# An inference step on one core: expert down matrices loaded as eight consecutive rows per partition, and `hid` turned by every eighth column

## The reference

```
g, idx = lax.top_k(aff.T, cap)
xe = xt[idx]
h = silu(einsum('ecd,edf->ecf', xe, w_gate)) * einsum('ecd,edf->ecf', xe, w_up)
ye = einsum('ecf,efd->ecd', h, w_down) * g[..., None]
out = zeros_like(xt).at[idx.reshape(-1)].add(ye.reshape(-1, D))
```

## Time and profile before

| | |
|---|---|
| median of 3 runs | 2083.78 us (2082.12 to 2083.93) |
| the profiled execution | 2084.59 us |
| its span | 2082.8 us |
| mean granted TensorE clock | 0.916 |
| busy: TensorE, VectorE, ScalarE, GpSimd | 1812.0, 1544.0, 1214.7, 570.5 us |
| HBM read | 496.90 MB |
| packets of the SP queue (q1) | 124288, 484.22 MB |

### The profile page before, as it was taken

How to read it: one execution, slowest core, us unless ns; L and a number is a source line. 1 busy time by engine, 2 the same in 40 slices (tenths; PEclk the granted TensorE clock), 3 DMA queues, 4 the chain that set the end, 5 groups by cost and what they waited for, 6 DMA issues and landing times.

```text
span 2082.8 us, 26307 instructions
## 1 busy us (share of the span) xinstructions
PE 1812.0 (87%) x8919; PEld 1265.4 (61%) x8919; DVE 1544.0 (74%) x1822; ACT 1214.7 (58%) x1518; POOL 570.5 (27%) x320
## 2 busy tenths in 40 slices
PE   1599969789999999999568789898699999999996
PEld 0388847656666666666357578777366666666664
DVE  0457663479999999999346376634699999999994
ACT  0356751168777777777241145522378777777774
POOL 0122230103434444342200050000223434434331
PEclk7699979599999999999779779997799999999997
DMA  9400271799999999999760330006399999999992
GB/s 342 137 1 1 83 292 48 299 339 366 361 375 358 378 359 378 362 378 365 189 134 0 128 121 1 1 1 269 135 361 376 359 378 359 376 357 378 365 376 83
DMA packets 139904, 519.04 MB, mean 249 GB/s; under 512 B 14944, under 2 KB 15232, under 8 KB 138815
## 3 DMA queue, kind: packets, MB, share of 16 engines
q1 hardware_dynamic: 124288, 484.22, 60.4%
q0 software_dynamic: 7216, 24.79, 6.2%
q10 hardware_dynamic: 8334, 9.17, 1.4%
HBM read 496.90 MB, written 21.24 MB: 249 GB/s over the span
## 4 chain that ended last, share of the span: by engine, by line
PE 55%; DVE 19%; issue 13%; ACT 5%; DMA 4%; ACTq 2%; POOL 1%; DVEq 0%; SPq 0%; POOLq 0%
PE ps L729 19%; PE ps L733 10%; DVE whl L1482 9%; PE ps L687 5%; PE ps L931 4%; PE ps L978 2%; ACT whl L1099 2%; DVE W L1513 2%; DMA ring<-in_at_w_qkv 2%; ACTq L1188 2%; PE ps L951 2%; PE ps L967 1%; PE ps L667 1%; PE ps L761 1%; DVE W L1500 1%
## 5 line engine op out<-in xcount | busy, mean ns | idle before, releaser
L1482 DVE TENSOR_TENSOR whl<-ring,whl 128x1024 fp32r<-128x1024 f32 x768 | 970.0, 1302 | 79.3 <-ACT whl L1099 66.7
L1099 ACT ACTIVATE whl<-ring 128x1024 fp32r<-128x1024 f32 x768 | 805.5, 1059 | 253.1 <-PE ps L733 234.9
L729 PE MATMUL ps<-whl,xs_hl 128*80 128x512 f32 x2048 | 561.0, 396 | 7.3 <-DVE xs_hl L1506 3.8
L729 PEld LDWEIGHTS ps<-whl,xs_hl 128*80 128x80 f32 x2048 | 298.7, 149 | 169.4 <-issue 6.2
L733 PE MATMUL ps<-whl,xs_hl 128*80 128x512 f32 x1024 | 323.3, 397 | 10.8 <-DVE whl L1482 7.5
L729 PE MATMUL ps<-whl,hs_hl 128*80 128x512 f32 x1024 | 280.9, 396 | 3.4 <-ACT hs_hl L1008 3.4
L532 POOL TENSOR_TENSOR W<-W 80x1024 f32<-80x1024 f32 x32 | 100.0, 3125 | 486.4 <-ACT W L1137 486.4
L733 PEld LDWEIGHTS ps<-whl,xs_hl 128*80 128x80 f32 x1024 | 147.6, 149 | 112.8 <-DVE whl L1482 37.9
L729 PEld LDWEIGHTS ps<-whl,hs_hl 128*80 128x80 f32 x1024 | 153.4, 150 | 89.3 <-ACT hs_hl L1008 3.8
L733 PE MATMUL ps<-whl,hs_hl 128*80 128x512 f32 x512 | 160.8, 396 | 0.0
L527 POOL COPY si<-idx_t 80x1 uint32 (+1 forms) x32 | 128.2, 4007 | 0.0
(11 more groups left out here) (253 smaller groups left out, 2508.7 us busy)
## 6 DMA issues: line engine op xcount, KB each, us to landing
ring<-in_moe_w_gate SPq DMA_DIRECT2D x128, 1024.0 KB, 6.7
ring<-in_moe_w_up SPq DMA_DIRECT2D x128, 1024.0 KB, 6.7
ring<-in_moe_w_down SPq DMA_DIRECT2D x128, 1024.0 KB, 6.1
ring<-in_mod_w SPq DMA_DIRECT2D x48, 1024.0 KB, 8.5
ring<-in_rg_w_in SPq DMA_DIRECT2D x8, 1024.0 KB, 15.0
ring<-in_at_w_qkv SPq DMA_DIRECT2D x8, 768.0 KB, 23.3
x_hat<-r ACTq DMA_DIRECT2D x2, 2560.0 KB, 18.9
ring<-in_rg_w_out SPq DMA_DIRECT2D x4, 1024.0 KB, 10.2
```

The source lines that it names most:

```text
L729: nc.tensor.matmul(ps[0:CE, bank + n, :], xhl[:, part, k, :], w[:, 0, n * 512:(n + 1) * 512], start=(k == 0 and part == 0), stop=False)
L1099: nc.scalar.activation(whl[:, q % HL, 0, :], ring[:, slot, (q % 2) * D:(q % 2 + 1) * D], ACT.Copy).then_inc(whi_ok, 1)
L1482: v.tensor_tensor(whl[:, q % HL, 1, :], ring[:, n % MSLOTS, (q % 2) * D:(q % 2 + 1) * D], whl[:, q % HL, 0, :].bitcast(F32), ALU.subtract) ...
```

## The change

The down matrices get a view of their own. Partition p now holds rows 8p to 8p + 7 of the 1024: slot s of the four of an expert's down matrix gets, for each partition, the consecutive rows 8p + 2s and 8p + 2s + 1, a single run of 8 KB in HBM, where there were two runs of 4 KB. From one partition to the next the source advances by 32 KB. So block k holds rows 8p + k. To match, transpose b takes `hid`'s columns b, b + 8, b + 16 and so on (128 of them). Gate and up loads are as before. No instruction changes its place on any engine; only the shape of the down loads and the step of the operand of these 256 transposes differ. Below `put` the line numbers grow by four, so L761 becomes L765.

```diff
             def load_moe(layer):
-                w3 = [w[layer].rearrange("e (k p) n -> p (e k) n", p=P) for w in (moe_w_gate, moe_w_up, moe_w_down)]
+                w3 = [w[layer].rearrange("e (k p) n -> p (e k) n", p=P) for w in (moe_w_gate, moe_w_up)]
+                down = moe_w_down[layer].rearrange("e (p k) n -> p e (k n)", p=P)

                 def put(slot, w, e, s):
-                    sp.dma_start(pair(slot), w3[w][:, bass.ds(e * KB + 2 * s, 2), :]).then_inc(slot_ready[slot], 16)
+                    if w < 2:
+                        sp.dma_start(pair(slot), w3[w][:, bass.ds(e * KB + 2 * s, 2), :]).then_inc(slot_ready[slot], 16)
+                    else:
+                        sp.dma_start(ring[:, slot:slot + 1, :], down[:, bass.ds(e, 1), 2 * s * D:2 * (s + 1) * D]).then_inc(slot_ready[slot], 16)
...
                     for b in range(KB):
-                        mm = nc.tensor.transpose(ps[:, 6 + b // 4, (b % 4) * CE:(b % 4 + 1) * CE], hid[0:CE, b * P:(b + 1) * P],
+                        mm = nc.tensor.transpose(ps[:, 6 + b // 4, (b % 4) * CE:(b % 4 + 1) * CE], hid[0:CE, b::KB],
                                                  ident[0:CE, 0:CE])
                     mm.then_inc(htr_mm, 1)
```

## The result

The changed kernel took 2094.21 us (median of 5, 2091.03 to 2097.39) against 2083.79 us (median of 5, 2082.12 to 2085.96) for the kernel before on the same chip: ratio 1.0047, 95% interval 1.0035 to 1.0058. That is 9.8 us slower by the ratio (0.0047 x 2083.8) and 10.4 us between the medians. Forecast were 2093.9 us and 10.1 us more.

What follows compares the result with a forecast made beforehand. The bound was a 35.87 us loop per expert through TensorE's matmuls, VectorE's chain and the turn of hid (L761). 2084.59 + 0 (loads) + 0 (packets) + 10.1 (turns) = 2094.7, 2093.9 us for the median; range 2081 to 2101.

Steps and rivals of the forecast that it cites:

- Loads: cost 0, gain 0: Down-matrix loads (L328): no rate gain from 8 KB runs, any gain hidden, 13.3 us spare at the slowest landing.
- Rival B: Ring of eight slots: reads 32 KB apart fall below 297 GB/s; at 250 GB/s 86 us more, 2170; chance 0.03.
- rival C: VectorE's L1482: fewer, longer packets disturb it less, saving 3.9 us, 2080 without a stride cost; with other gains, chance 0.07.
- Packets beside the loads: 0.8 us, hidden: Gathers on GpSimd's queue: waiting behind 8 KB packets adds 0.8 us, hidden by 3.4 us spare; cost 0.
- The strided load: Turns of hid (L761): weight load with a 32-byte step takes 0.111 us, 0.34 us more per expert, 10.1 us in all.
- the middle: Turns of hid: 10.1 us chosen between the ends of 0 and 36.7 us for the strided load's cost.
- the half of the plain load's time: Turns of hid: a side-by-side transpose load assumed at 0.055 us, about half the plain fp32 load's 0.111 us.
- Rival A: Turns of hid: the strided load stays hidden under the 80 moving columns, 2083.8 us, no change; chance 0.38.
- The turn is on the loop, in full: L761, each expert once: whatever lengthens the turn lengthens each 35.87 us period by the same amount.
- The turns at the lower clock are free: Last turn of each layer, clock 0.50: starts 0.133 us apart hide a 0.111 us load, so 30 of 32 turns count.
- Sum: Whole kernel: 2084.59 + 0 + 0 + 10.1 = 2094.7 us for the profiled execution, 2093.9 for the median.
- 3.4 us to spare: Gather on GpSimd's queue: issued 10.2 us before the turn of its rows (L752), for a landing of 6.8 us.

Runs made afterwards that it cites:

- loads_only: The changed kernel's loads of the down matrices with the old turn of side-by-side columns: 2083.59 us, ratio 0.9995 to the kernel before.
- turns_twice: The kernel before with the eight transposes of hid made twice in a row: 2099.77 us, ratio 1.0086.
- perm_write: The changed kernel, but VectorE writes hid in the order of the down rows and the turn reads side-by-side columns: 2104.83 us, ratio 1.0102.
- before_k3: The kernel before with the turn of hid one gate block later, after k == 3 in place of k == 2: 2094.53 us, ratio 1.0049.

## Why the prediction was right

- **Loads: cost 0, gain 0.** Right, by loads_only. Issue and landing of the down loads were measured at 333 ns and 5.2 to 6.6 us. Rival B (reads 32 KB apart) and rival C (less disturbance of VectorE) are gone with it.
- **Packets beside the loads: 0.8 us, hidden.** The cost was not seen. With the changed loads alone a gather landed after 6.8 us, as before. With the whole change it took 8.4, but with the strided turn alone 8.2. So it comes with the turn and not from packets: GpSimd's issue of a gather took 2.8 us with the strided turn, where it took 1.1 to 1.3 before. It was covered because the gather was also issued earlier, some 14.5 us before its turn in place of 10.2.
- **The strided load.** Taken at 0.111 us per transpose, measured 0.108; 8 x 0.042 = 0.34 us per expert, measured 751.89 - 750.98 = 0.91 us from the turn's start to the next block against 746.40 - 745.83 = 0.57 in the kernel before (the block's row is in the section on the result), 0.34. Right in size. The reason that I gave for taking the middle was weaker than the number: I expected a rate that a step of eight cannot keep up, and the same slowing is there at a step of two. And the half of the plain load's time and its doubling by the stride, from which the middle value came, were guesses that no run measured: how long the side-by-side load is by itself is still unknown. That the size came out to 0.003 us is in part luck. Rival A is refuted.
- **The turn is on the loop, in full.** Right: the period rose by 0.33 us, and turns_twice and perm_write put 0.55 and 0.73 us more at this place and found 0.55 and 0.72 in the period. This was the step that could most easily have gone wrong, since TensorE waits 0.55 us just before the turn, and a wait invites the thought that it hides something.
- **The turns at the lower clock are free.** Right for layer 0: 1.33 us in both kernels. In layer 1 the changed kernel's turn took 1.20, at a mean granted clock of 0.80, so there it shows nothing.
- **Sum.** 30 x 0.33 = 9.9 us by the measured period, 9.8 by the ratio, 10.1 forecast. From the first to the last turn, each layer grew by 5.1 us (layer 0: 1002.41 - 461.36 = 541.05 against 994.88 - 458.90 = 535.98), 10.2 in both.

What the forecast did not see is how near the gather was to the loop. I reckoned 3.4 us to spare from one place of its issue; before_k3 lost all of it by moving one turn by one block. Which side of GpSimd's copies and issues a longer or later turn falls on was in no term of the sum; that the changed kernel came out on the good side of it (it issued its gathers earlier) was not foreseen.

## What to carry to other kernels

Find the loop that sets the period, in the chain of waits, and ask what stands on it once per round; a wait on it is not slack for the work behind it. Longer runs in a load pay only if the load is waited for: here the loads had 13 us to spare, and the rearrangement that they asked for had to be paid on the loop, as a strided operand on TensorE (0.34 us per expert) or on VectorE (0.73). Before an order is changed on one engine, look at which small instructions on the others get through only at certain moments, and at what waits for them.

## What the runs showed of the hardware

- A transpose's weight load of 128 fp32 columns started every 0.069 us with side-by-side columns, where the moving side of 80 columns may have set the pace, every 0.108 us with a step of eight and every 0.116 us with a step of two (granted clock 1.00). The step's size hardly mattered; that it was not one did.
- A VectorE product of 80x1024 that writes with a step of 512 bytes took 1.94 us against 1.21.
- A GpSimd copy of 80x1 took from 0.18 to 12.12 us, depending on what VectorE ran beside it. In the kernels with the later turn it got through at L1521 (L1517) whenever ScalarE's share was ready 0.13 us or more after the start of the subtraction before (56 cases), and never when it was ready within 0.07 us of it (48 cases).
- Loads with 8 KB per partition, 32 KB apart, cost no time against loads with two runs of 4 KB (ratio 0.9995, 0.9986 to 1.0004): 6.3 us at the median from issue to landing against 5.9.
